# The weights of the 16 meta tokens in the second mixer's attention units, as 16 rows in place of 128

## What is computed

```python
# differential attention, 8 heads of 2 x 64, values of 128
a = softmax(s1 + bias) - lam * softmax(s2 + bias)      # (256, 272) a head
o = a @ v                                              # (272, 128) values a head
# grouped-query attention with rotary positions, 8 heads of 128 on 2 key heads
p = softmax(q @ k.T * scale)                           # (256, 272) a head
o = p @ v
```

## Time and profile before

| what | value |
|---|---|
| time, median of 3 runs | 1920.42 us (1920.09 to 1922.02) |
| the profiled execution's own time | 1919.19 us |
| its span, first to last instruction | 1917.4 us |
| mean granted TensorE clock | 0.997 of full speed |
| instructions | 33984 |
| TensorE matmul busy | 1889.7 us, 99% of the span |
| TensorE weight load busy | 1752.5 us, 91% |
| VectorE busy | 1101.7 us, 57% |
| ScalarE busy | 914.2 us, 48% |
| GpSimd busy | 178.9 us, 9% |

### The profile page before, as it was taken

How to read it: one execution, slowest core, us unless ns; L and a number is a source line. 1 busy time by engine, 2 the same in 40 slices (tenths; PEclk the granted TensorE clock), 3 DMA queues, 4 the chain that set the end, 5 groups by cost and what they waited for, 6 DMA issues and landing times.

```text
span 1917.4 us, 33984 instructions
## 1 busy us (share of the span) xinstructions
PE 1889.7 (99%) x13468; PEld 1752.5 (91%) x13468; DVE 1101.7 (57%) x1265; ACT 914.2 (48%) x1189; POOL 178.9 (9%) x135
## 2 busy tenths in 40 slices
PE   9999999999999999999999999999999999998998
PEld 9989998999999889988998899899889998888986
DVE  6655766466655555554545545554566457766664
ACT  6534444565644455443443344344454354655543
POOL 2001331401000100000010000000010000031000
PEclk9999999999999999999999999999999999999999
DMA  8665656566565656666656666566555554444454
GB/s 272 191 180 171 185 179 177 152 193 177 171 220 186 208 187 177 196 199 189 196 187 198 190 195 194 190 183 202 188 185 173 175 170 133 116 136 144 133 187 143
DMA packets 176435, 346.49 MB, mean 181 GB/s; under 512 B 10976, under 2 KB 11184, under 8 KB 175776
## 3 DMA queue, kind: packets, MB, share of 16 engines
q1 hardware_dynamic: 174176, 337.76, 57.0%
q0 software_dynamic: 2128, 6.82, 1.4%
HBM read 342.44 MB, written 2.10 MB: 180 GB/s over the span
## 4 chain that ended last, share of the span: by engine, by line
PE 94%; DVE 3%; ACT 2%; issue 1%; DMA 0%; SPq 0%; POOL 0%; DVEq 0%; ACTq 0%
PE ps L430 56%; PE ps L442 32%; DVE wlo L1240 1%; ACT whi L857 1%; PE ps L758 1%; PE ps L527 1%; PE ps L745 1%; PE ps L722 0%; PE ps L460 0%; DMA x_nat<-in_x_dram 0%; PE ps L733 0%; PE ps L578 0%; PE ps L696 0%; DVE p L1652 0%; PE ps L570 0%
## 5 line engine op out<-in xcount | busy, mean ns | idle before, releaser
L1240 DVE TENSOR_TENSOR wlo<-raw,whi 128x1024 fp32r<-128x1024 f32 x631 | 804.1, 1280 | 719.3 <-ACT whi L857 718.3
L857 ACT ACTIVATE whi<-raw 128x1024 fp32r<-128x1024 f32 x631 | 664.1, 1058 | 872.6 <-PE ps L430 545.1
L430 PE MATMUL ps<-xhi,whi 128*128 128x256 f32 (+1 forms) x1984 | 567.3, 286 | 0.0
L430 PE MATMUL ps<-xhi,wlo 128*128 128x256 f32 (+1 forms) x1984 | 555.4, 280 | 0.0
L430 PE MATMUL ps<-xlo,whi 128*128 128x256 f32 (+1 forms) x1952 | 546.8, 280 | 0.0
L430 PEld LDWEIGHTS ps<-xhi,whi 128*128 128x128 f32 x1984 | 375.0, 189 | 10.0 <-issue 7.6
L430 PEld LDWEIGHTS ps<-xhi,wlo 128*128 128x128 f32 x1984 | 373.8, 188 | 0.0
L430 PEld LDWEIGHTS ps<-xlo,whi 128*128 128x128 f32 x1952 | 368.8, 189 | 1.5 <-issue 0.7
L430 PE MATMUL ps<-x2hi,whi 128*128 128x256 f32 x1024 | 282.8, 276 | 0.0
L430 PE MATMUL ps<-x2lo,whi 128*128 128x256 f32 x1024 | 282.7, 276 | 0.0
L430 PE MATMUL ps<-x2hi,wlo 128*128 128x256 f32 x1024 | 282.7, 276 | 0.0
(11 more groups left out here) (357 smaller groups left out, 2220.6 us busy)
## 6 DMA issues: line engine op xcount, KB each, us to landing
raw<-in_w_in_dram SPq DMA_DIRECT2D x279, 512.0 KB, 3.8
raw<-in_w_up_dram SPq DMA_DIRECT2D x128, 512.0 KB, 3.8
raw<-in_w_down_dram SPq DMA_DIRECT2D x128, 512.0 KB, 3.7
raw<-in_w_out_dram SPq DMA_DIRECT2D x64, 512.0 KB, 4.0
raw<-in_w_branch_a_dram SPq DMA_DIRECT2D x16, 512.0 KB, 4.2
raw<-in_w_branch_b_dram SPq DMA_DIRECT2D x16, 512.0 KB, 4.1
x_nat<-in_x_dram SPq DMA_DIRECT2D x4, 512.0 KB, 7.0
rel<-in_rel_turned_dram POOLq DMA_DIRECT2D x8, 256.0 KB, 4.4
```

Source lines behind the costliest of these rows:

```text
L430: ins = mm(outs[b], w[:, k % SLOTS, j, cols], v, start=start, stop=last and j == CK - 1 and i == 2, skip_group_check=True)
L857: f(whi[:, k % SLOTS], raw[:, k % SLOTS], ACT.Copy).then_inc(whi_ready, 1)
L1240: tt(wlo[:, k % SLOTS], raw[:, k % SLOTS], whi[:, k % SLOTS], ALU.subtract).then_inc(wlo_ready, 1)
```

## The change

The third transpose of `weights_turn` takes the 16 meta columns alone and writes 16 partitions. The third product of `values` takes 16 rows of both operands. The zeros of `v_meta`, their semaphore and the two waits for it go. What ACT copies to `pt2` stays as it is, 128 partitions by 384 columns; of its last 128 columns only the first 16 partitions are read.

```diff
@@ program
-        vm_zero = sem("vm_zero")
@@ weights_turn, TensorE
-                for i in range(3):
-                    ins = nc.tensor.transpose(ps[:, 6, i * P:(i + 1) * P], p[:, i * P:(i + 1) * P], ident[:])
-                ins.then_inc(u_t, 1)
+                for i in range(2):
+                    nc.tensor.transpose(ps[:, 6, i * P:(i + 1) * P], p[:, i * P:(i + 1) * P], ident[:])
+                nc.tensor.transpose(ps[0:META, 6, T:T + P], p[:, T:TM], ident[:]).then_inc(u_t, 1)
@@ values, TensorE
-                parts = (v_nat[:, vh, 0, :], v_nat[:, vh, 1, :], v_meta[:, vh, :])
+                parts = (v_nat[:, vh, 0, :], v_nat[:, vh, 1, :], v_meta[0:META, vh, :])
                 for i, v in enumerate(parts):
-                    w = pt2[:, u % 2, i * P:(i + 1) * P]
+                    w = pt2[0:META if i == 2 else P, u % 2, i * P:(i + 1) * P]
                     l, r = (w, v) if u < B_UNITS else (v, w)
                     ins = mm(ps[:, 7, 0:P], l, r, start=i == 0, stop=i == 2)
@@ values_copy, ScalarE and VectorE
-                act.wait_ge(vm_zero, 1)
-                dve.wait_ge(vm_zero, 1)
@@ GpSimd
-            nc.gpsimd.memset(v_meta[:], 0.0).then_inc(vm_zero, 1)
```

## The result

The changed kernel took 1928.42 us (median of 6 runs, 1925.11 to 1931.7) against 1919.76 us for the kernel before (6 runs, 1917.02 to 1922.02). The ratio is 1.0045, with a 95% interval of 1.0035 to 1.0056: slower by about 8.7 us, between 6.7 and 10.8. The profiled execution has a span of 1927.1 us against 1917.4, 9.7 us more, at the same mean clock of 0.997.

A forecast was written before the change was run, and what follows sets the result against it. PE was taken to bound the kernel, with 94% of the last-ending chain. Entering 6.1 us plus leaving 5.0 less 0.3 hidden gave 10.8 us, so 1931.2 us against the runs' median; range 1926.0 to 1935.0 us.

The forecast's parts named there:

- The mechanism: Third product of each of 32 units: two array switches, each delaying the next start by 0.09 us and exposing a load.
- The no-switch rival: Third product: 16 rows may run on the full array, PE's starts unchanged, 1920.4 us; chance 0.11.
- the faster one: Third product and transpose: fewer rows or columns go through sooner, 4.6 us saved, 1915.8 us; chance 0.03.
- The third transpose and the memset: Shorter transpose load stays hidden, and removing the POOL memset and its waits changes nothing: no time.
- Entering: Going into the 16-row product: 0.09 us delay plus 0.10 us exposed load, 0.19 us; 32 entries make 6.1 us.
- leaving: After the 16-row product: 0.15 us into line 745, 0.18 us into a chunk or line 733; 5.0 us in all.
- 0.26 us a round trip: Line 482's 16-row pieces between chunks, taken to show that 16 rows behave as 64 do; would give 8.3 us.
- The waits: Two exits ahead of PE's 1.2 us waits for DVE are hidden, -0.3 us; the entries there are not hidden.
- The rival in which the waits swallow 3.3 us more: Two shorter waits of line 745 (2.4 us) and the copy's 0.9 us vanish, 1927.9 us; chance 0.12.
- My count of PE's waits: Unit stage: line 745 waits for DVE 6.9 us, line 758 for its copy 0.9 us, together 7.8 of 240 us.
- The clock: Rival: border gaps added to waits at 1765 and 1800 bring two more clock falls, 2.4 us, 1933.6 us; chance 0.08.
- The waits of rows 3 where they were: Sign for the profile after: PE's waits for DVE at lines 745 and 758, 7.8 us together, stay where they were.

The follow-up runs named there:

- e2: Kernel before with only the third product cut to 16 rows; transpose, memset and its waits stay: 1929.39 us, ratio 1.0049.
- e3: Kernel before with the third product over 68 rows, 16 of values and 52 of zeros: 1921.21 us, ratio 1.001.
- e4: Kernel before with the third product over 64 rows, 16 of values and 48 of zeros: 1930.45 us, ratio 1.0051.
- e7: Kernel before, but in 12 B positions the third product goes over 64 rows, right ahead of the 64-row scores: 1919.59 us, ratio 1.0.
- e1: Kernel before with only the third transpose cut to 16 columns; third product stays at 128 rows: 1919.05 us, ratio 0.9996.
- e8: As e7, but the product moved ahead of the scores goes over 16 rows: 1923.74 us, ratio 1.0012 against the kernel before.

## Why the prediction was right, and where it was off

**The mechanism** was the one forecast, a delay and a late load on each side of the product: e2 puts the whole loss there, e3 and e4 show the step, e7 shows it gone when the neighbour has 64 rows too. That the array is switched inside is a reading of these delays, which no run looks into. The no-switch rival (0.11) and the faster one (0.03) are excluded.

**The third transpose and the memset: nothing.** e1 has 0.9996.

**Entering, 0.19 us; leaving, 0.15 or 0.18 us.** Line 757's 16-row pair starts 0.54 us after the first of `v_nat`, where it was 0.44 before (1611.66 to 1612.10), and takes 0.41 us instead of 0.23; the exposed load of the transposes is the last 0.06. That makes 0.10 + 0.18 + 0.06 = 0.34. A unit with a transpose behind it costs 0.34 us, as forecast. The five with a chunk or line 732 behind them cost 0.34 to 0.385 by position, where I had 0.37. Lines 722, 570 and 572 at 64 rows were the right neighbours; line 482, with 0.26 us a round trip, was the wrong one although it alone had 16 rows. That its 16-column passes hide part of the price is likely, and no run shows it.

**The waits: this term was mis-sized.** I let 0.3 us fall into them, "Two of the 27 lie ahead of the 1.2 us waits for DVE", and wrote "The entry ahead of those waits is not hidden, since DVE copies `values` out before it normalises". But the copy that stands ahead of that normalisation is of the position before: DVE is a position behind, late by a group's gate work, and comes to this position's result only after the normalisation for which PE waits. Three whole units are in the shadow at each place, and "None falls into a wait", said of the 32 entries, does not hold for six of them: 2 x 3 x 0.34 = 2.0 us. With that the sum is 6.1 + 5.0 - 2.0 = 9.1 us. At the `values` behind the rope product of position 17 the change costs 0.18 us and not 0.34: there a first matmul already started late. That leaves 8.9 us, the sum by position. The median moved by 8.7 us. The rival in which the waits swallow 3.3 us more had the right place and too large a size: the two shorter waits of the transposes did not vanish, they went from 1.17 to 0.99 us, while the copy's did. By its number, 1927.9 us, it was nearer to the measured 1928.42 than my 1931.2, of which 0.7 us come from a kernel before that now has 1919.76 and not 1920.42. My count of PE's waits, 7.8 us, also left out two of the stage, 1.8 us at line 696 and 1.0 at line 722; they hid nothing of the change, since both are as long after the change.

**The clock.** The rival wanted two more falls behind the short waits; in the trace of the full change there was none. The one fall of the unit stage that both kernels have, behind the long wait, lasted longer in this execution, about 1 us of the profile's 9.7. In e1, whose code there is that of before but for a shorter load, the same stretch is 0.6 us longer than before, so this length varies by itself. Five of the experiments' traces have one fall more, at line 696 (see e2), which was not forecast. All five kernels have short products without a neighbour of the same height, but so has the full change, whose trace has no such fall. The rival's mechanism is therefore not excluded, and the cause of that fall stays open.

**What of the signs forecast came.** Loads together with their matmuls, 0.34 us a B position, the third load at 90 ns without effect: yes. From the first pass of 16 rows to the second 0.21 us, and "from there to line 745 0.20": yes, 0.41 for both. "The waits of rows 3 where they were": no, and that was the mis-sized term.

## What to carry to other kernels

Zeros around a short product can be the cheap choice. On an engine that is the bound, two passes of 128 columns took 0.23 us over 128 or 68 rows and 0.41 us over 64 or 16, and the whole detour cost 0.34 to 0.385 us, since at each change between these groups the next matmul started 0.09 us late and its load, 0.06 to 0.10 us of it, was not hidden. 68 rows in place of 128 saved nothing. If rows must be few, put the product beside others of the same number: 64 beside 64 cost nothing (e7), 16 beside 64 cost 0.19 us (e8). And before writing off a cost as hidden or not, follow the late engine's chain back to where it starts: all that the bound engine does from there on is in its shadow.

## What the runs showed that I had not expected

- Leaving 16 rows for 64 takes as long as leaving them for 128: from the start of the pair of passes to the next matmul it is 0.41 us in e8 and in the full change alike. The Trainium skill (TensorEngine Tiling (Array Packing), Key Properties) says that a change of tiling mode drains the engine; e8 is the case within row tiling, and it agrees.
- A transpose with 16 stationary columns stays on the whole array (0.11 us pace, loads ahead, e1), while the program's products with 64 stationary columns, line 589, start 0.21 us behind the chunk before them. It looks as if the columns of a transpose and those of a product are not treated alike; no run changed the columns of a product.
- In e7 one pass of the scores starts 0.01 us behind the product's first pass and ahead of its second, although the program has it behind. The view doesn't name the half; that it is the one on rows 64 to 127, which the product leaves free, is the likely reading. In the trace before, the passes of the two halves of line 722 start in pairs, 0.01 us apart. The total stayed the same.
- DVE's normalisation took 2.06 us instead of 0.36 at each of the two places; a POOL operation of 3.2 us ran beside each, from 1763.73 and from 1798.26. That the one slows the other was not tried.
